# Choosing experts for two heads at a time, with one wait per row, in a fused two-block transformer kernel

## The reference, cut to what matters

```python
q = (xt @ wq).reshape(t, 8, 2, 128)
scores = jnp.einsum('thpd,hpnd->thpn', q, keys)          # 8 heads, 2 halves, 128 keys
s_top, i_top = lax.top_k(scores, 16)
cand = (s_top[:, :, 0, :, None] + s_top[:, :, 1, None, :]).reshape(t, 8, 256)
c_score, c_idx = lax.top_k(cand, 16)
i1 = jnp.take_along_axis(i_top[:, :, 0], c_idx // 16, axis=-1)
i2 = jnp.take_along_axis(i_top[:, :, 1], c_idx % 16, axis=-1)
expert = i1 * 128 + i2                                   # one of 16384
gates = jax.nn.softmax(c_score, axis=-1)
# per token and each of its 128 chosen experts k:
a = gelu(x . u_tab[expert_k]);  y += gates_k * a * v_tab[expert_k]
```

## Time and profile before

| what | us |
|---|---|
| median of 3 runs (lowest, highest) | 2591.3 (2580.96, 2597.47) |
| the profiled execution, its own time | 2577.69 |
| its span | 2575.9 |
| PE busy (86%) | 2217.4 |
| DVE busy (62%) | 1608.4 |
| POOL busy (36%) | 934.2 |
| ACT busy (24%) | 618.5 |

### The profile page before, as it was taken

The page is one execution under the profiler, slowest core; times in us unless marked ns, Lnnn a source line. Parts: engine busy times, 40 slices in busy tenths (PEclk is TensorE's granted clock), DMA queues, the critical chain, the costliest instruction groups (busy, mean ns, idle before and its releaser), DMA issues.

```text
span 2575.9 us, 25112 instructions
## 1 busy us (share of the span) xinstructions
PE 2217.4 (86%) x8844; PEld 1559.3 (61%) x8844; DVE 1608.4 (62%) x3632; ACT 618.5 (24%) x1793; POOL 934.2 (36%) x772
## 2 busy tenths in 40 slices
PE   7999999999989998898999988876533599999992
PEld 6877768846858886676687646745432544444440
DVE  0122312202536778899677776968998999866667
ACT  1223212202212112422111112011798810000000
POOL 0000000000003344454356565536567356555544
PEclk9979999999989976898999999888655799999996
DMA  5522344444338886787899999969679589999997
GB/s 165 149 90 90 107 143 159 147 147 136 131 106 302 277 277 234 273 301 267 289 343 397 392 383 329 336 231 358 215 247 364 171 329 409 409 409 408 406 409 277
DMA packets 296691, 683.55 MB, mean 265 GB/s; under 512 B 21235, under 2 KB 134131, under 8 KB 296309
## 3 DMA queue, kind: packets, MB, share of 16 engines
q0 software_dynamic: 110592, 402.70, 42.2%
q1 hardware_dynamic: 179904, 266.54, 30.1%
q10 hardware_dynamic: 6068, 12.71, 1.5%
HBM read 679.78 MB, written 2.10 MB: 265 GB/s over the span
## 4 chain that ended last, share of the span: by engine, by line
PE 45%; DVE 25%; DMA 16%; POOL 7%; issue 4%; ACT 2%; ACTq 0%; DVEq 0%
PE bank L624 43%; DVE SLOT L1743 9%; DMA SLOT<-in_peer_v,EI 9%; POOL SLOT L2288 7%; DMA SLOT<-in_peer_u,EI 7%; PE bank L651 2%; DVE ACC L1757 2%; DVE X L1757 1%; DVE H L1675 1%; DMA W<-in_w_up 1%; DVE PB L1295 1%; PE bank L776 1%; DVE OH L1644 0%; DVE OH L1648 0%; DVE I L1601 0%
## 5 line engine op out<-in xcount | busy, mean ns | idle before, releaser
L2288 POOL DMA_INDIRECT SLOT<-in_peer_u,EI x512 | 643.3, 1256 | 1350.3 <-DVE T L1597 793.3
L624 PE MATMUL bank<-HT,W 128*128 128x256 f32 x4032 | 915.8, 388 | 18.1 <-issue 8.7
L624 PEld LDWEIGHTS bank<-HT,W 128*128 128x128 f32 x4032 | 775.7, 194 | 136.5 <-issue 18.6
L1743 DVE CUSTOM_DVE_ANT_0 SLOT<-SLOT,H 128x1024 f32<-128x1024 f32 x384 | 455.0, 1220 | 43.4 <-DMA SLOT<-in_peer_u,EI 41.0
L2288 POOL DMA_INDIRECT SLOT<-in_peer_v,EI x256 | 290.7, 1135 | 268.4 <-DVE ACC L1757 122.1
L624 PE MATMUL bank<-H,SPREAD 128*128 128x512 f32 x680 | 304.7, 598 | 4.9 <-DMA H<-in_peer_v 4.5
L624 PEld LDWEIGHTS bank<-H,SPREAD 128*128 128x128 f32 x680 | 125.0, 190 | 178.8 <-issue 129.0
L1757 DVE SCALAR_TENSOR_TENSOR X<-SLOT,AA,X 128x1024 f32<-128x1024 f32 x128 | 164.4, 1284 | 79.1 <-DMA SLOT<-in_peer_v,EI 76.6
L1743 DVE CUSTOM_DVE_ANT_0 SLOT<-SLOT,ACC 128x1024 f32<-128x1024 f32 x128 | 153.4, 1221 | 41.3 <-DMA SLOT<-in_peer_u,EI 41.1
L1757 DVE SCALAR_TENSOR_TENSOR ACC<-SLOT,AA,ACC 128x1024 f32<-128x1024 f32 x128 | 164.1, 1282 | 20.0 <-DMA SLOT<-in_peer_v,EI 13.2
L624 PE MATMUL bank<-JK,SPREAD 128*128 128x512 f32 x344 | 156.2, 597 | 1.7 <-DMA JK<-in_peer_v 1.6
(11 more groups left out here) (304 smaller groups left out, 2390.3 us busy)
## 6 DMA issues: line engine op xcount, KB each, us to landing
W<-in_w_in SPq DMA_DIRECT2D x68, 1024.0 KB
W<-in_w_up SPq DMA_DIRECT2D x44, 1024.0 KB
H<-in_peer_v SPq DMA_DIRECT2D x85, 512.0 KB
JK<-in_peer_v SPq DMA_DIRECT2D x43, 512.0 KB
W<-in_w_down SPq DMA_DIRECT2D x20, 1024.0 KB
W<-in_peer_wq SPq DMA_DIRECT2D x16, 1024.0 KB
W<-in_w_o SPq DMA_DIRECT2D x8, 1024.0 KB
W<-in_w_out SPq DMA_DIRECT2D x8, 1024.0 KB
```

Source lines behind the costliest of these rows:

```text
L624: return e.matmul(out, lhsT, rhs, start=start, stop=stop)
L1743: e.tensor_tensor_reduce(out=x, in0=x, in1=NORMED[t], scale=1.0, scalar=0.0, op0=ALU.mult, op1=ALU.add, accum_out=AA[t % 2][:, k:k + 1]).t ...
L2288: e.indirect_dma_start(out=SLOT_OF[s], out_offset=None, in_=a["peer_v_2"] if i >= P else a["peer_u_2"], in_offset=bass.IndirectOffsetOnAxi ...
```

## The change

`best`, `pairs` and `numbers` each take two heads. `top_sixteen` marks every row by itself, so that a row's next stage waits for the same row's last stage only: `best` works on four rows (two heads, two halves), `pairs` on two. In `numbers` each instruction takes both heads (64 rows of 16 in place of 32), and the one-hot rows lie in 16-bit unsigned integers; expert numbers of a pair are released together, so that POOL waits for those of 32 jobs. `best` waits for the scores of the second head of its pair. The planner's costs are 5.0, 4.3 and 4.4 for two heads in place of 3.0 each for one. `LEAD` lies behind three pairs (six heads) in group 0 with 20 jobs, and behind two pairs (four heads) with 14 jobs in group 1; before it lay behind three heads with 13 jobs in both.

```diff
-HEAD = ("best", "pairs", "numbers")
+HEAD = {"best": 5.0, "pairs": 4.3, "numbers": 4.4}
...
-    head = [[(part, t, h, 3.0) for h in range(8) for part in HEAD] + [("picked", t, 0, 0.3), ("gates", t, 0, 0.7)]
+    head = [[(part, t, h, HEAD[part]) for h in range(0, 8, 2) for part in HEAD] + [("picked", t, 0, 0.3), ("gates", t, 0, 0.7)]
...
-    for h in range(8):
-        for n in (2, 2, 2 if h == 1 else 3):
+    for h in range(0, 8, 2):
+        for n in (4, 5, 5) if g or h != 4 else (2, 2, 2):
             steps.append(head[0].pop(0))
             if h:
                 steps += [jobs[0].pop(0) for _ in range(n)]
-        if h == 2:
+        if h == (2 if g else 4):
             LEAD.append(len(steps))
-            if g:
-                steps.append(("halves", DENSE[0], 0, 1.0))
+        if g and h == 2:
+            steps.append(("halves", DENSE[0], 0, 1.0))
+            steps += [spreads[0].pop(0) for _ in range(2)]
         elif g and h > 2:
-            steps += [spreads[0].pop(0) for _ in range(2 if h == 3 else 3)]
+            steps += [spreads[0].pop(0) for _ in range(6)]
...
-            if later and n % 5 == 0:
+            if later and n % 10 == 0:
...
-            if later and (n < 3 or n > 5 and n % 4 == 2):
+            if later and (n < 3 or n > 5 and n % 8 == 2):
...
+        PAIR = [buf(f"PAIR{j}", 256) for j in range(2)]
+        OH = buf("OH", 64, 16, at=pair_at, dt=U16)
...
-                    if step[0] == HEAD[0]:
-                        catch_up("top", g, step[2])
+                    if step[0] == "best":
+                        catch_up("top", g, step[2] + 1)
...
-                for v, ix, s in jobs:
-                    k = e.max(v[:, 0:8], s)
-                k.then_inc(*d_exp.mark(*name, "m1"))
-                w.wait_ge(*d_exp[name + ("m1",)])
-                for v, ix, s in jobs:
-                    k = e.max_index(ix[:, 0:8], v[:, 0:8], s)
-                k.then_inc(*d_exp.mark(*name, "i1"))
+                for j, (v, ix, s) in enumerate(rows):
+                    e.max(v[:, 0:8], s).then_inc(*d_exp.mark(*name, "m1", j))
+                for j, (v, ix, s) in enumerate(rows):
+                    w.wait_ge(*d_exp[name + ("m1", j)])
+                    e.max_index(ix[:, 0:8], v[:, 0:8], s).then_inc(*d_exp.mark(*name, "i1", j))
...
-                e.tensor_tensor(one_hot, HL.rearrange("p s j -> p (s j)").unsqueeze(2).to_broadcast([P, 32, 16]),
-                                IOTA[:, 0:16].unsqueeze(1).to_broadcast([P, 32, 16]), ALU.is_equal).then_inc(
+                e.tensor_tensor(OH, HL.unsqueeze(2).to_broadcast([P, 64, 16]),
+                                IOTA[:, 0:16].unsqueeze(1).to_broadcast([P, 64, 16]), ALU.is_equal).then_inc(
...
-                e.tensor_copy(EI[t % 2][:, 16 * h:16 * h + 16], IX).then_inc(*d_exp.mark("index", t, h))
+                e.tensor_copy(EI[t % 2][:, 16 * h:16 * h + 32], IX.rearrange("p l j -> p (l j)")).then_inc(
+                    *d_exp.mark("index", t, h))
...
-                    w.wait_ge(*d_exp["index", t, k // 16])
+                    w.wait_ge(*d_exp["index", t, k // 32 * 2])
```

More of the change, by code:

```diff
@@ L11 @@
 U32 = mybir.dt.uint32
+U16 = mybir.dt.uint16
 AX = mybir.AxisListType.X
@@ L304, in build, with buf @@
         top = [0]
-        def buf(name, *shape, at=None):
+        def buf(name, *shape, at=None, dt=F32):
             n = prod(shape)
+            words = n if dt == F32 else n // 2
             if at is None:
                 at = top[0]
-                top[0] += (n + 7) // 8 * 8
-            assert at % 8 == 0 and at + n <= WORDS, (name, at, n)
-            v = nc.alloc_sbuf_tensor_at(name, [P, n], F32, offset=ORIGIN + 4 * at)[:, :]
+                top[0] += (words + 7) // 8 * 8
+            assert at % 8 == 0 and at + words <= WORDS, (name, at, words)
+            v = nc.alloc_sbuf_tensor_at(name, [P, n], dt, offset=ORIGIN + 4 * at)[:, :]
             if len(shape) == 2:
@@ L1616, in best @@
             def best(g, t, h):
-                w.wait_ge(*a_qry["top", g, h])
+                w.wait_ge(*a_qry["top", g, h + 1])
                 if h == 0 and t % GB:
                     w.wait_ge(*d_exp["picked", t - 1])
-                top_sixteen(("top", t, h), [(T16[:, half, :], I16[:, half, :], SCORED[t][:, h, half, :])
-                                            for half in range(2)])
+                top_sixteen(("top", t, h), [(T16[:, j, half, :], I16[:, j, half, :], SCORED[t][:, h + j, half, :])
+                                            for j in range(2) for half in range(2)])
@@ L1624, in pairs @@
             def pairs(t, h):
-                w.wait_ge(*d_exp["top", t, h, "i2"])
-                e.tensor_copy(IF, I16)
-                e.tensor_tensor(PAIR.rearrange("p (a b) -> p a b", a=16), T16[:, 0, :].unsqueeze(2).to_broadcast(
-                    [P, 16, 16]), T16[:, 1, :].unsqueeze(1).to_broadcast([P, 16, 16]), ALU.add).then_inc(
-                        *d_exp.mark("pair", t, h))
-                w.wait_ge(*d_exp["pair", t, h])
-                top_sixteen(("best", t, h), [(CSC[:, h, :], CIX[:, h, :], PAIR)])
+                for j in range(2):
+                    w.wait_ge(*d_exp["top", t, h, "m2", 2 * j + 1])
+                    e.tensor_tensor(PAIR[j].rearrange("p (a b) -> p a b", a=16),
+                                    T16[:, j, 0, :].unsqueeze(2).to_broadcast([P, 16, 16]),
+                                    T16[:, j, 1, :].unsqueeze(1).to_broadcast([P, 16, 16]), ALU.add).then_inc(
+                                        *d_exp.mark("pair", t, h, j))
@@ L1634, in numbers @@
+                w.wait_ge(*d_exp["top", t, h, "i2", 3])
+                e.tensor_copy(IF, I16.rearrange("p l s a -> p (l s) a"))
+                w.wait_ge(*d_exp["pair", t, h, 1])
+                top_sixteen(("best", t, h), [(CSC[:, h + j, :], CIX[:, h + j, :], PAIR[j]) for j in range(2)])
             def numbers(g, t, h):
-                w.wait_ge(*d_exp["best", t, h, "i2"])
-                e.tensor_scalar(HLI[:, 0, :], CIX[:, h, :], 4, None, ALU.logical_shift_right)
-                e.tensor_scalar(HLI[:, 1, :], CIX[:, h, :], 15, None, ALU.bitwise_and).then_inc(
+                w.wait_ge(*d_exp["best", t, h, "i2", 1])
@@ L1639, in numbers @@
+                e.tensor_scalar(HLI[:, :, 0, :], CIX[:, h:h + 2, :], 4, None, ALU.logical_shift_right)
+                e.tensor_scalar(HLI[:, :, 1, :], CIX[:, h:h + 2, :], 15, None, ALU.bitwise_and).then_inc(
                     *d_exp.mark("hli", t, h))
                 w.wait_ge(*d_exp["hli", t, h])
[L1641 removed]
+                e.tensor_copy(HL, HLI.rearrange("p l s j -> p (l s j)")).then_inc(*d_exp.mark("hl", t, h))
                 w.wait_ge(*d_exp["hl", t, h])
[L1643 removed]
@@ L1657, in numbers @@
                 if g:
-                    last = t - GB, (0 if t - GB in DENSE else P) + 16 * h + 15
+                    last = t - GB, (0 if t - GB in DENSE else P) + 16 * h + 31
                     w.wait_ge(*slot_in[slot_of(g - 1, number(*last))][("job",) + last])
-                e.tensor_copy(EI[t % 2][:, 16 * h:16 * h + 16], IX).then_inc(*d_exp.mark("index", t, h))
+                e.tensor_copy(EI[t % 2][:, 16 * h:16 * h + 32], IX.rearrange("p l j -> p (l j)")).then_inc(
+                    *d_exp.mark("index", t, h))
             def spread(t, q):
@@ L1717, in expert @@
                     gw = GW[t % 2].rearrange("p (h j) -> p h j", h=8)
-                    w.wait_ge(*d_exp["best", t, 7, "m2"])
+                    w.wait_ge(*d_exp["best", t, 6, "m2", 1])
                     if t >= GB:
```

43 lines of the change are left out of this document (19 added, 24 removed).

## The result

| | before | after |
|---|---|---|
| median, us (lowest to highest, runs) | 2587.0 (2581.0 to 2597.5, 4) | 2620.9 (2610.2 to 2629.0, 4) |
| the profiled execution, us | 2577.7 | 2610.2 |
| its span, us | 2575.9 | 2608.4 |
| DVE busy, us | 1608.4 | 1565.2 |

The ratio is 1.0124 (95% interval 1.0070 to 1.0179). The kernel became slower by 34 us (18 to 46 by the interval), just over what I called measurable; the forecast was 2595, and 2621 lies at the upper edge of its range, 2568 to 2620. DVE has 43 us less work, as meant, and the time went up all the same.

What follows compares the result with a forecast made beforehand. Bounds: PE, closely DVE, in group 1's attention; DMA in mlp; DVE and ACT from 1819 to 2016; PE with DMA in the tail. Terms +26, +3, -22, -3 sum to +4: median 2591.3 becomes 2595 us, range 2568 to 2620.

Steps and rivals of the forecast that it cites:

- first rival: ACT's spreads of tile 1: late halves or gathers holding ACT; second queries return only 8 to 10; 2618 us, chance 0.23.
- step 3: Second queries of group 1 up to tile 2's weights: PE's 22.5 us stop goes; -22 us, bounds -30 and -10.
- The price of a pair: Best, pairs and numbers on DVE: two heads together cost 14.2 us against 18.1.
- Step 1: Six heads beside the first queries: the longer lead delays project(1) on PE; +26 us, bounds 20 and 36.
- step 2: Group 1's project, attention, mlp and mixer: +3 us, from +4 in mlp, 0 in project, 1 credited in attention.
- Step 4: Tile 2's spreads and the tail: heads' savings hidden by DMA, POOL waits less; -3 us, bounds -6 and +2.
- The second: Lead and attention: cheaper numbers shorten the lead, PE's idle time halves, second queries give 30; 2568 us, chance 0.17.
- The third: Best and pairs on DVE: waits per row win nothing, a pair costs 16.7; +16 us, 2607 us, chance 0.06.

Runs made afterwards that it cites:

- e5: The changed kernel, but each stage of best and pairs waits for the last row of the stage before; median 2624.6 us, ratio 1.0159 to the kernel before.
- e1: The changed kernel, but group 0's lead ends behind two pairs (four heads, 14 jobs); median 2572.1 us, ratio 0.9964 to the kernel before.
- e2: The changed kernel, but tile 2's gates step comes 30 jobs after picked in place of 6; median 2600.4 us, ratio 1.0077 to the kernel before.
- e6: The changed kernel, but group 0's gathers fetch 512 elements in place of 1024, read twice by DVE; median 2582.3 us, ratio 1.0000 to the kernel before.
- e6b: The kernel before, but group 0's gathers fetch 512 elements in place of 1024, read twice by DVE; median 2563.6 us, ratio 0.9930 to the unedited kernel before.
- e3: The changed kernel, but planner costs of 6.0 for each pair step in place of 5.0, 4.3, 4.4; median 2587.0 us, ratio 1.0031 to the kernel before.
- e10: The changed kernel with four-head lead, late gates, early halves, and the tail's second-pair steps behind jobs 0, 4, 8; median 2562.0 us, ratio 0.9908.

## Why the prediction was right or wrong

The direction of the sum was right, its size was not: +32.5 by stage where it said +4. The time of 2621 is that of its first rival (2618), and reached at other places than the rival named; that the range reached so far was owed to that rival, and so in part luck. By its own test, that the time from the second queries to the tail shrinks by less than 12 us (it shrank by 6.6, 346.8 to 340.2), it was wrong; more executions make this test less sure (step 3).

**The price of a pair: right.** 14.0 against 14.2, and the lever is the one named: waits cost where no other row covers them, 0.13 each (e5). The Trainium skill (VectorE: DVE Perf Modes, "The DRAIN you can't avoid") has the next operation wait for the pipe with a semaphore or without, but also says that one that is not held starts earlier. For these instructions the rows don't agree: a chain of MAX8 of 0.28 us starts one every 0.20, and a wait for the last row of four adds 0.12 to that for the first. The 16-bit rows brought nothing and cost nothing, as taken; the 0.3 for a conversion, its upper bound, had no row behind it and shows in none.

**Step 1, the lead, +26: right.** +24.4, and 18 of them go with the third pair (e1). It had been priced as if it ended with its own time, though; see step 2.

**Step 2, +3: the mis-sized term.** It measured +10.1. The mlp gave +4.3, the +4 of the sum; the miss is project to merge, +5.6 where -1 stood, and +11.6 by e2's execution. The step that failed is "in project DVE had 20 us of slack and DMA some room: 0". I counted 23 more jobs up to the mlp by their DVE time, which is nothing, and took their bytes only in the mlp, where the DMA share is 0.99. With 0.81 and 0.84 over the stage, DMA is not full on average, and loads of weights still come late beside more gathers: with half the bytes the loss was 0.9 and no weight was late (e6, e6b). A share below 1 over 450 us hides stretches where a weight is late, and the wait of 9.86 us for in_cmp_k_w is one; 4.5 of it is new, since DVE held this product for 5.4 before.

**Step 3, -22: the places right, the size open.** The stop went, and tile 1's weights came 19.3 earlier (forecast 19; 75.0 to 75.6 in e1, e2, e3 and e6). DVE's wait for the exponential was 12.6 (forecast 12). What was too small is "80 jobs (92) + pair 13.8 + some waits on gathers", taken from a kernel in which ACT and DVE ended together. From the gates to the transposes it took 131 us where 111 had been put, and 119.5 to 129.0 in e1, e3 and e6, which have the same steps. Of the 20 us in the changed kernel's execution, 13.0 are waits on gathers (the forecast had some 5 in its 111) and 5.6 the pauses named "remote" or standing beside them.

How much of the 22 came back can't be read from one pair of executions. From the second queries to the tail the changed kernel took 340.2, and e1, e3 and e6 337.5, 330.2 and 328.6; the kernel before took 346.8 and e6b, with the same steps there, 356.6. The means, 334 and 352, lie 18 apart: near the forecast, where the one pair says 6.6. So the +12.7 between the weights of tiles 1 and 2 in the table of the result is not shown to come from the change. What removing the wait gives back is 12 to 13 us, and not the whole 25 of its pair (e2).

In the changed kernel's execution ACT was done with its spreads at 2018 and then waited 24.1 us for DVE, where the kernel before waited 2.8. But e6b, with that kernel's steps, has 25.1 here, so this too is not shown to come from the change:

```profile
2043.31 0.31 ACT L2238 ACTIVATE AA<-AA 128x128 f32<-128x128 f32 x1 [24.08 <-DVE AA L1748]
```

**Step 4, -3: wrong in sign.** +4.5; all tails with the changed steps took 507.9 to 512.7, the kernel before 505.4 and e6b 505.1. "Hidden by DMA" was the error: the three steps of 4.7 us stand close together at the start of the tail, hold POOL's slots and its next numbers, and 36 GB/s of 359 are missing for 50 us. At 409 GB/s, which later slices show, that is 4.4 us. e10 undid it.

**The rivals.** The first said that halves would land late, or that gathers would hold up ACT. Neither happened; its outcome came from DMA under project, from the tail, and from DVE between the weights, the last by this execution alone. The second, a cheaper lead and cheaper numbers, had nothing for it. The third is refuted by e5.

## What to carry to other kernels

An instruction stream that gets cheaper on one engine lets the queue behind it run ahead: count what is fetched earlier, in bytes, against what shares the transfer engines at that time, and not only where their share reads 1. Larger pieces on an engine that frees buffers need to be spread, since each one stops the queue that it feeds for its whole length. A planner with fixed costs has a cliff where its list no longer fits: here between 750 and 776 of planned work, worth a stop of 15 us and 12 to 19 at the next product that counts. And before a difference of 12 us in one stage is explained, look how far that stage varies between executions that do the same there: here by 12.

## What the runs showed of the hardware

A gather on POOL takes 0.94 us while DVE stands, and up to 1.99 beside a row of dot products. DVE and POOL of the changed kernel in order of time:

```profile
1903.73 0.94 POOL L2293 DMA_INDIRECT SLOT<-in_peer_u,EI  x1 [0.30 <-issue]
...
1917.51 1.22 DVE L1748 CUSTOM_DVE_ANT_0 SLOT<-SLOT,H 128x1024 f32<-128x1024 f32 x1
1917.55 1.99 POOL L2293 DMA_INDIRECT SLOT<-in_peer_u,EI  x1 [0.30 <-issue]
...
1919.80 1.22 DVE L1748 CUSTOM_DVE_ANT_0 SLOT<-SLOT,H 128x1024 f32<-128x1024 f32 x1
1919.85 1.99 POOL L2293 DMA_INDIRECT SLOT<-in_peer_u,EI  x1 [0.30 <-issue]
...
1922.09 1.22 DVE L1748 CUSTOM_DVE_ANT_0 SLOT<-SLOT,H 128x1024 f32<-128x1024 f32 x1
1922.13 1.98 POOL L2293 DMA_INDIRECT SLOT<-in_peer_u,EI  x1 [0.30 <-issue]
```

The two run in step: each gather begins 0.04 us after a dot product has begun and lasts into the next one, so POOL issues one for every two jobs, 2.28 apart, while DVE uses one every 1.15. That can let DVE, after its stop, run out of gathered rows. The length follows from where in a dot product the gather begins: 1.99 at its start, 1.68 at 0.4 us, 1.40 at 0.6, some 1.25 at 0.8 and 0.95 from 1.1 on, as if its 0.94 us began only when the dot product ends. Of the 310 gathers of this trace that begin within a dot product, 295 follow this to within 0.1 us; 10 of the others begin in its first 0.04 us and take 0.94. The dot products keep their 1.22 us.

Beside an instruction with a single input in SBUF a gather is not lengthened. DVE and POOL of the kernel before:

```profile
1681.38 1.75 DVE L1501 RECIPROCAL T<-T 128x256 f32<-128x256 f32 x1
1681.73 0.93 POOL L2288 DMA_INDIRECT SLOT<-in_peer_u,EI  x1 [1.92 <-DVE AA L1743]
```

It begins 0.35 us into the reciprocal, and takes 0.93 us where the same place in a dot product gives 1.7.

The Trainium skill (SBUF — State Buffer, "SBUF: two separate sides") has DVE and GpSimd share a pair of ports as a lock: it is taken by a DVE instruction in a two-port mode, or by one with two inputs in SBUF, the latter only against a GpSimd operation that reads SBUF, and the first to come holds it for its whole instruction. The trace agrees for POOL's side: the dot product has two inputs in SBUF (the slot and the features), the gather reads its expert numbers from there, and it waits. It does not show the other side: a gather's last 0.9 us run beside the next dot product, which takes 1.22 us all the same. No run changed the inputs alone, so the cause is argued from this contrast.

Instructions of 1024 elements with 16-bit numbers on one side or on both ran 1.22 us, at the rate of 32-bit ones.
